# The first attention of a two-block network: stacked queries and keys, outputs already transposed, weights scaled by GpSimd

## What is computed

```python
s = jnp.einsum('btgrd,btgkd->btgrk', q_b, k_sel) * ATTN_SCALE
p = masked_softmax(s, mask)
...
g = jax.nn.sigmoid(gate_logits.astype(jnp.float32)).reshape(B, S, G, R, 3).astype(o_cmp.dtype)
o_nsa = g[..., 0:1] * o_cmp + g[..., 1:2] * o_sel + g[..., 2:3] * o_win
o_nsa = o_nsa.reshape(B, S, NSA_WIDTH) * jax.nn.silu(z_n)
...
o_dsa = o_dsa.reshape(B, S, DSA_WIDTH) * jax.nn.silu(z_d)
mixed = jnp.concatenate([o_nsa, o_dsa], axis=-1)
return x + jnp.einsum('bsc,cd->bsd', mixed, w_out)
```

## Time and profile before

| | |
|---|---|
| median of three runs | 1795.41 us |
| the profiled execution: its own time / span of the trace | 1794.89 us / 1793.1 us |
| busy: TensorE / VectorE / ScalarE / GpSimd | 97% / 55% / 41% / 39% |
| first turns of keys to the first score | 192.2 to 199.3 us |
| units of the first attention | 199.3 to 363 us |
| gate, turns, halves | 363 to 371.1 us |
| output projection `o1` | 371.1 to 425.5 us |

### The profile page before, as it was taken

One profiled execution on the slowest core, in us unless ns is written; L12 is line 12 of the kernel. 1 busy time (PEld: TensorE's weight loads), 2 busy tenths in 40 slices (PEclk: granted clock), 3 DMA queues, 4 the chain that ended last, 5 costly groups with the idle time before them and its releaser, 6 DMA issues. The chain is left out here.

```text
span 1793.1 us, 23296 instructions
## 1 busy us (share of the span) xinstructions
PE 1735.9 (97%) x8345; PEld 1416.5 (79%) x8345; DVE 990.4 (55%) x1657; ACT 741.1 (41%) x1282; POOL 694.3 (39%) x301
## 2 busy tenths in 40 slices
PE   7999998988999999999999999999999999999997
PEld 7777787777888777788888888887777888888886
DVE  5999776474579688633333335789775731111112
ACT  6434555523375564322222223466465343122321
POOL 3424111235430234555445557440211644444442
PEclk9999999999999999999999999999999999999998
DMA  7234010053332224455555532332310323232311
GB/s 251 82 106 141 24 36 25 24 194 121 109 101 100 83 83 149 146 193 192 189 193 194 188 141 94 108 103 84 106 37 24 106 94 100 90 104 94 99 54 47
DMA packets 56633, 197.65 MB, mean 110 GB/s; under 512 B 6993, under 2 KB 8017, under 8 KB 56530
## 3 DMA queue, kind: packets, MB, share of 16 engines
q1 hardware_dynamic: 55666, 194.15, 31.6%
q10 hardware_dynamic: 864, 2.11, 0.3%
HBM read 194.14 MB, written 2.10 MB: 109 GB/s over the span
## 5 line engine op out<-in xcount | busy, mean ns | idle before, releaser
L516 POOL TENSOR_TENSOR WL<-RAW,WH 128x1024 fp32r<-128x1024 f32 x234 | 593.9, 2543 | 872.6 <-ACT WH L600 535.9
L1917 PE MATMUL bank<-HH,WH 128*128 128x512 f32 x1120 | 439.0, 392 | 9.1 <-POOLq L521 5.4
L1919 PE MATMUL bank<-HH,WL 128*128 128x512 f32 x1120 | 437.7, 391 | 0.0
L1918 PE MATMUL bank<-HL,WH 128*128 128x512 f32 x1120 | 437.7, 391 | 0.0
L600 ACT ACTIVATE WH<-RAW 128x1024 fp32r<-128x1024 f32 x259 | 270.6, 1051 | 246.0 <-PE bank L1919 220.0
L1917 PEld LDWEIGHTS bank<-HH,WH 128*128 128x128 f32 x1120 | 211.5, 189 | 54.7 <-issue 8.0
L1919 PEld LDWEIGHTS bank<-HH,WL 128*128 128x128 f32 x1120 | 211.4, 189 | 44.1
L1918 PEld LDWEIGHTS bank<-HL,WH 128*128 128x128 f32 x1120 | 211.4, 189 | 43.6
L1837 DVE TENSOR_TENSOR HF<-SILU,bank 128x512 f32<-128x512 f32 x43 | 29.6, 688 | 301.6 <-PE bank L1919 300.6
L1917 PE MATMUL bank<-HDH,WH 128*128 128x512 f32 x352 | 137.1, 390 | 0.0
L1919 PE MATMUL bank<-HDH,WL 128*128 128x512 f32 x352 | 137.0, 389 | 0.0
(11 more groups left out here) (371 smaller groups left out, 2933.5 us busy)
## 6 DMA issues: line engine op xcount, KB each, us to landing
RAW<-in_stream SPq DMA_DIRECT2D x363, 512.0 KB, 3.3
out_t<-YA SPq DMA_DIRECT2D x8, 256.0 KB, 2.2
X<-in_xt ACTq DMA_DIRECT2D x3, 512.0 KB, 10.8
RAW<-in_stream SPq DMA_DIRECT2D x2, 256.0 KB, 3.9
X<-in_xt ACTq DMA_DIRECT2D x2, 256.0 KB, 6.0
ACC<-in_pos SPq DMA_DIRECT2D x1, 256.0 KB
gains<-in_gains SPq DMA_DIRECT2D x1, 224.0 KB
CS<-in_cs SPq DMA_DIRECT2D x1, 128.0 KB
```

The lines of the kernel that those rows point to most:

```text
L516: nc.gpsimd.tensor_tensor(lo(k)[:], raw(k)[:], hi(k)[:].bitcast(F32), ALU.subtract).then_inc(sem["passed"], mark("passed", *k))
L1917: nc.tensor.matmul(out, A[0], B[0], start=first, stop=False)
L1918: nc.tensor.matmul(out, A[0], B[1], start=False, stop=False)
L1919: return nc.tensor.matmul(out, A[1], B[0], start=False, stop=last)
```

## The change

- `UNITS1` goes head by head: four tiles of a head in one branch, then the other branch; the third branch last, head by head.
- The queries of a head are stored twice over 128 partitions, the rounded half on 64 and the rest on the other 64 (in `HH` and `HL`, free in this stage); a key head is stored as its rounded half on both 64s (in `WH`) and its rest on both (in `WL`). A score is two one-pass products. The compressed keys are done likewise (`KCS`).
- GpSimd scales each unit's weights by reciprocal sum and gate before they are turned (VectorE makes one reciprocal per unit); it also takes over the scaling of the first eight `ada` slots. The ring of weights grows from 4 to 8, the lags from 3 and 4 to 6 and 8.
- The values lie in `VZ` with 64 zero columns between heads, so that the output of a head can be added on either half of a bank. A pair of heads, both branches and the compressed branch gather in one bank (`pair_bank`), channels-first, from four products per head and branch.
- The gate `Z` is turned instead of the outputs (`GATE_TURN`), VectorE multiplies each finished pair with it, ScalarE and GpSimd (the last two: VectorE) make the halves.
- Of the turns before the loop only four stay; the others and the stacking are spread over the first 60 units (`TURNS`, `CONVERT`). Zeroing of `KT` (GpSimd) goes; `VZ` is zeroed at the kernel's start.
- The first two tiles of `o1` begin inside the loop (`O1_PARTS`); the sixteen `ada` slots beside `o1` all stand behind its third slot.

```diff
-        order += [ada.pop(0) for _ in range((2, 3, 3, 3, 3, 2, 0, 0)[n])]
+        order += [ada.pop(0) for _ in range((0, 0, 4, 4, 4, 4, 0, 0)[n])]
...
-UNITS1 = [(b, j, g, qt) for b in (0, 1) for j in range(4) for qt in range(NT) for g in range(2)]
-UNITS1 += [(2, j, g, qt) for qt in range(NT) for j in range(4) for g in range(2)]
+UNITS1 = [(b, h % 4, h // 4, qt) for h in range(HEADS) for b in (0, 1) for qt in range(NT)]
+UNITS1 += [(2, h % 4, h // 4, qt) for h in range(HEADS) for qt in range(NT)]
+RING1, T_LAG1, O_LAG1 = 8, 6, 8
...
+O1_PARTS = {101: ((0, 0, 3),), 102: ((0, 3, 5),), 103: ((0, 5, 7), (1, 0, 7), (0, 7, 8), (1, 7, 8))}
+GATE_TURN = {14 + 6 * c: c for c in range(KD)}
+TURNS = {5: ("tqn", 1), 8: ("tqn", 2), 11: ("tqn", 3), 13: ("tkc",)}
+TURNS.update({38 + 6 * j: ("tqd", j) for j in range(4)})
+CONVERT = {0: (("tk", 0, 1),), 1: (("tqn", 0, 1),), 2: (("tk", 1, 0),), 3: (("tk", 1, 1), ("tk", 2, 0)),
+           4: (("tk", 2, 1),), 13: (("tkc",),)}
+CONVERT.update({5 + 3 * (j - 1) + g: (("tqn", j, g),) for j in range(1, 4) for g in range(2)})
+CONVERT.update({38 + 6 * j + g: (("tqd", j, g),) for j in range(4) for g in range(2)})
...
+            for v in range(len(UNITS1)):
+                br, j, g, qt = UNITS1[v]
+                n = (qt + 1) * P
+                pool.wait_ge(sem["p_inv"], value("p_inv", v))
+                p_, over = PR[v % RING1][:, 0:n], COEF1[:, v % 16:v % 16 + 1]
+                if br == 2:
+                    ins = nc.gpsimd.tensor_scalar(p_, p_, over, ones[:, 0:1], ALU.mult, ALU.mult)
+                else:
+                    col = 3 * (4 * g + j) + 1 + br
+                    ins = nc.gpsimd.tensor_scalar(p_, p_, over, gate[:, qt, col:col + 1], ALU.mult, ALU.mult)
+                ins.then_inc(sem["p_pool"], mark("p_pool", v))
+                if v - 1 in ATT_ADA:
+                    pass_to(SLOT[("ada", 0, ATT_ADA.index(v - 1))] + 1)
...
+                if kind == "tk":
+                    k_hi, _ = key_stack(i, g)
+                    nc.scalar.activation(k_hi[rows_of(1 - g), :], b, ACT.Copy)
+                    ins = nc.scalar.activation(k_hi[rows_of(g), :], b, ACT.Copy)
+                else:
+                    ins = nc.scalar.activation(query_stack(kind, 4 * g + i)[rows_of(g), :], b, ACT.Copy)
...
-                    nc.tensor.matmul(b[:, 0:n], (QNT if br < 2 else QDT)[:, j, qt * P:(qt + 1) * P],
-                                     KT[:, 2 * br + g, 0:n], start=True, stop=False)
+                    for i, part in enumerate(key_stack(br, g)):
+                        nc.tensor.matmul(b[:, 0:n], query_stack(kind, 4 * g + j)[:, qt * P:(qt + 1) * P],
+                                         part[:, 0:n], start=(i == 0), stop=False)
...
-                        last = nc.tensor.matmul(b, PT1[:, v % RING, kb * P:(kb + 1) * P],
-                                                G[4][:, kb, c:c + DH], start=(kb == 0), stop=(kb == qt))
+                        last = nc.tensor.matmul(
+                            pair_bank[c][:, kb * P:S], VZ[:, kb, DH * m:DH * m + P], PT1[e % 2][:, kb, kb * P:S],
+                            start=(kb == 0 and NT * e == first),
+                            stop=(kb == NT - 1 and c >= 4 and NT * e + NT - 1 == end))
```

More of the change, by code:

```diff
@@ L227 @@
 RING = 4
-def evictor(v):
-    return "read_dve" if v % 4 == 3 else "read_act"
 UNITS2 = [(h, qt) for h in range(HEADS) for qt in range(NT)]
@@ L437, in first_square, with rows_of, query_stack, key_stack @@
             return (RELU[:, 0, :], RELU[:, 1, :], TMP[:, 0, :], TMP[:, 1, :])[k % 4]
+        def rows_of(g):
+            return slice(DH * g, DH * g + DH)
+        def query_stack(kind, h):
+            return (HH if kind == "tqn" else HL)[:, h, :]
+        def key_stack(br, g):
+            cols = slice(S * g, S * g + S)
+            return WH[KEY_SLOT[br]][:, cols], WL[KEY_SLOT[br]][:, cols]
+        def gated(c):
+            return Z[:, :, c * P:(c + 1) * P]
+        def chunked(x, c):
+            return x[:, c, :].rearrange("p (t q) -> p t q", t=NT)
         block = ctx.enter_context(nc.Block())
@@ L1511, in _ @@
+            pair_at = {pair_done(c) + 1: c for c in range(KD)}
             nU = len(UNITS1)
-            for u in range(nU + O_LAG):
+            for u in range(nU + O_LAG1):
                 if u < nU:
@@ L2156, in _, with turned @@
-            for i in range(4):
-                turn(("tqd", i), [G[3][:, tt, i * P:(i + 1) * P] for tt in range(NT)])
+            def turned(kind, i=0):
+                if kind == "tkc":
+                    pe.wait_ge(step, value("cmp_key"))
+                    turn(("tkc",), [CK[0:2 * NCMP, 0, :]], rows=DH)
+                    return
+                group = {"tk": 1, "tqn": 2, "tqd": 3}[kind]
+                pe.wait_ge(step, value("roped", group))
+                turn((kind, i), [G[group][:, tt, i * P:(i + 1) * P] for tt in range(NT)])
@@ new lines, in o1_part @@
+            def o1_part(n, k0, k1):
+                slot = ("o1", n)
+                if k0 == 0:
+                    o1_bank[n] = claim(*slot)
+                    pe.wait_ge(sem["passed"], value("passed", *slot))
+                for k in range(k0, k1):
+                    last = mm3(o1_bank[n][:], wpair(slot, P * k, P), mix_pair(k), k == 0, k == KD - 1)
+                if k1 == KD:
+                    full(last, *slot)
+                    used(slot)
+            o1_bank, pair_bank = {}, {}
@@ L2168, in _ @@
+            for u in range(nU + O_LAG1):
+                mods(("att", u))
+                if u in TURNS:
+                    turned(*TURNS[u])
+                c = GATE_TURN.get(u)
+                if c is not None:
+                    turn(("tz", c), [Z[:, tt, c * P:(c + 1) * P] for tt in range(NT)])
                 qt = cmp_tile(u, 0)
                 if qt is not None:
+                    pe.wait_ge(sem["read_dve"], value("read_dve", "tkc"))
                     for g in range(2):
@@ new lines, in _ @@
+                for c in range(4):
+                    if u == pair_done(c):
+                        if c == 0:
+                            pe.wait_ge(sem["read_act"], value("read_act", "ct", NT - 1))
+                        full(nc.tensor.matmul(pair_bank[c][:], VBLK[:, c // 2, P * (c % 2):P * (c % 2) + P],
+                                              PTC[:, c // 2, :], start=False, stop=True), "oc", c)
+                for n, k0, k1 in O1_PARTS.get(u, ()):
+                    o1_part(n, k0, k1)
@@ L2238, in _ @@
+            banks[0] = 8
             for n in range(KD):
-                dense(("o1", n), [(("o1", n), P * k) for k in range(KD)], mix_pair)
+                if n > 1:
+                    dense(("o1", n), [(("o1", n), P * k) for k in range(KD)], mix_pair)
                 mods(("o1", n))
```

368 lines of the change are left out of this document (204 added, 164 removed).

## The result

The changed kernel takes **1831.1 us** (median of four, 1826.8 to 1835.2), the kernel before 1796.1 beside it: ratio 1.0197, 95% interval 1.0172 to 1.0222. It is slower by 35 us; the forecast of 1774 missed by 57.

What follows compares the result with a forecast made beforehand. The prediction took TensorE's instruction list, plus about 10 us of waits, to bound the first attention. Its terms, -25.9 + 4.6 + 1.3 - 4.6 - 5 + 2.0 + 9.8 - 3 = -20.8 us, gave 1774 from 1794.9; range 1757 to 1789.

Steps and rivals of the forecast that it cites:

- Filling: First units of the attention loop: ScalarE's stacking leaves TensorE 7.8 us idle, plus 2 us for half clock; +9.8 us.
- Waits in the loop: First attention's loop: the others catch up during a head's block of output products, so fewer waits; -3 us.
- coupling rival: Loop: six banks leave less slack and every unit takes 0.16 us more, 15 us in all, 1789 us; chance 13%.
- Scores: First attention: two one-pass products per score, 1.30 us for four tiles in place of 2.38, 24 times; -25.9 us.
- Outputs: First attention: a head's output products take 2.25 us in place of 2.06, 24 times; +4.6 us.
- compressed scores: First attention: they stay 64 instructions, at 0.12 us each in place of 0.10; +1.3 us.
- Seam: Between attention and output projection: 8.1 us go, 32 gate turns of some 3.5 us move into the loop; -4.6 us.
- Projection: Output projection: clock stays at 1.0, two slots are split in advance, 4 us of waits left; -5 us.
- Start: Before the loop: first score at about 198.1 instead of 199.3, and 29 turns costing 3.2 us move behind it; +2.0 us.
- GpSimd's scaling: Loop: GpSimd scales each unit's weights in 0.33 to 0.76 us, costed at nothing; bounds 0 to +4 us.
- on GpSimd: Rival: GpSimd's scaling in every unit's chain becomes the bound; at 1.6 us a unit the kernel takes about 1815; chance 5%.
- slow products: Rival: one-pass products are no faster at these shapes, the scores' gain becomes 0 and the time 1800; chance 2%.

Runs made afterwards that it cites:

- e4: The changed kernel without the stacking of keys and queries in units 0 to 12, except the first key head and query; 1800.5 us, ratio 1.0018.
- e2: The changed kernel with VectorE making the low halves of a stack one unit later in units 0 to 9, behind the next maximum; 1820.6 us, ratio 1.0140.
- e1: The changed kernel with 60 filler products of TensorE in the holes of the first 12 units, written to banks nobody reads; 1833.4 us, ratio 1.0193.
- e9: The changed kernel with the second branch's late queries turned into the free output bank and their low halves made behind the next maximum; 1818.4 us, ratio 1.0136.
- e3: The changed kernel with the four output products of a head and branch spread over three units for the first 16 groups; 1825.1 us, ratio 1.0163.
- e13: The changed kernel with the edits of e4, e3, e9 and e12 together (stacking of the first units left out); 1776.2 us, ratio 0.9888.
- e12: The changed kernel with the modulation's slots beside the projection two or three at a time instead of four by four; 1830.5 us, ratio 1.0184.
- e7: The changed kernel with all eight banks in rotation until unit 11, instead of six; 1832.6 us, ratio 1.0203.
- e6: The changed kernel without GpSimd's 96 scalings of the weights (that work is left out); 1828.7 us, ratio 1.0186.
- e10: The changed kernel with the edits of e2, e3 and e9, third key stacked later, four banks until unit 4, two top-8 rounds moved into the loop; 1799.2 us.
- e14: e10 plus four key moves and table load ahead, e12's slot order, late queries turned two units later, first modulation turns five later; 1788.5 us, ratio 0.9957.

## Why the prediction was wrong

- **Filling (+9.8, bounds 3 to 13): the step that failed.** e4 puts the stacks of the first units at 30.6 us, or 25.1 by the trace. The key that I had ready for unit 4 at 206.3 is ready at 211.45, and unit 11, forecast at 213.8, is scored at 233.3. I had followed ScalarE's list by hand, moves and exponentials, and had let VectorE run beside it. In the order of the program VectorE's low halves stand ahead of the next maximum and wait for ScalarE's moves, and the next exponential waits for that maximum: nothing overlaps, 3.6 us from one exponential to the next with a key (of the 30.6, e2's order alone is 10.5). Both orders stood in the kernel's text; what was missing was to follow two in-order lists together. The half clock that I priced at 2 us lasted through most of the stretch, but it was free (e1).
- **Waits in the loop (-3, bounds +5 to -8): failed too, and by the trace this is the larger part.** From the first outputs to the last it takes 176.5 us, forecast 141; scores and outputs make 4.5 of these 35. Late stacks cost 12.7 us (e9), the outputs in a block 6.0 (e3), and with both mended and the first stacks gone e13's loop takes 149.2. I had noted the block and taken it for a place where the others catch up; they ran dry instead. A granted clock well below 1.0 in the loop, which I had named as a sign of being wrong, came: 0.89 from 240 to 360 us. The coupling rival named the six banks, as 0.16 us in every unit; the loss sat in few places, where a stack stands in the way, by its order or by the bank it holds (e9).
- **Scores (-25.9): mis-sized.** 1.58 us for four tiles make it 24 x (1.58 - 2.38) = -19.2. The first of the two products takes more than the second (0.15 against 0.11, 0.31 against 0.24), and I had read only the last one of a unit in the other attention.
- **Outputs (+4.6):** 2.16 in place of 2.25 us, +2.4. The compressed scores were right (16 products in 1.93 us).
- **Seam (-4.6): right.** The chain runs on without a gap: projection products begin at 405.85 and again at 411.45 directly behind the outputs, at a clock of 1.00 from 400 to 420 us. (At 3.22 us for 28 the 32 turns are 3.7 us, not 3.5.)
- **Projection (-5): the gain didn't come.** 51.9 us from the last outputs, and 3.5 for 15 products before them, 55.4 against 55 before. The waits of 4.8 us are those I left room for; what I counted on, a clock near 1.0, was 0.93. e12's order gets 3.9 of it in the stage, and nothing in the kernel's time.
- **Start (+2.0): near.** First score at 200.2, forecast 198.1; in kernels that leave the start alone it lay between 197.7 (e4) and 200.7 (e7), 199.3 in the mean.
- **GpSimd's scaling (0): right** (e6: 2.4 us less without it, within the noise).
- **Range and slack.** All bounds on the slow side together (+3.2, +8, +5, +4) give 1794, and the range ended at 1789. Three units of 1.44 us are 4.3 us of slack; the 3.7 of the coupling rival doesn't follow from them.

The slower side had 6%, most of it on GpSimd and 2% on slow products. It should have had the stacks: the one piece of new work that stands in a dependent chain while the pipeline is still empty. That e13 lands at the forecast is in part luck: its first outputs come 4 us earlier than forecast, since the filling is left out, and its loop takes 8 us longer, of which the scores are 6.7.

Open: whether in e9 the bank or the order did more; and why four executions of the changed kernel spread over 8 us, where four of the kernel before spread over 3. The two long ones (1835) have a mean granted clock of 0.972, the two short ones (1827) 0.975 and 0.978; what sets it isn't shown.

## What to carry to other kernels

When a change adds a step that crosses two in-order engines (one rounds, the other subtracts), follow both lists together at the place where it stands, and ask what the next item of each list waits for: a conversion that the pipeline doesn't need for many units belongs behind the next unit's work on the second engine, not ahead of it. A piece of data parked in a rotating bank shortens the rotation for everybody; park it in one that is out of the rotation (e9 shows the gain only together with a better order, and more banks alone, e7, brought nothing). And a half clock beside an idle TensorE is first of all a sign: look for the chain that it waits for before paying for filler.

## What the runs showed of the hardware

The granted clock of TensorE stayed near the lower level for most of 40 us while it was busy half of the time (20.1 of 40 us, 0.53), and filler products of bf16 in the holes brought it to 0.83 (27.4 of 40 us). From 240 to 360 us it was 0.89, and TensorE's longest waits there are the four of 15.4 us together. Behind the wait of 5.3 us at 312.91 a product of 384 columns takes 0.49 us to the next start, behind the one of 3.0 us at 327.87 the next such product (329.22) takes 0.26, as at full clock. The Trainium skill ("TensorE: Matmul & The Clock Gate", section "A second HAM failure mode: psum-queue depth-cycling") describes another case, a kernel whose clock swings since it cycles through banks and idles very briefly between groups of products; no run here shows that. An edit of order alone moved the clock of fixed stretches (which then hold other units) both ways: e3 brought 240 to 300 us from 0.89 to 0.97 and 300 to 360 from 0.89 to 0.83; e12 brought the projection from 0.93 to 1.00 and the 20 us behind it from 1.00 to 0.83.

The first exponential after the sine carried a load of its table. In e10, and then in e14, where an instruction of its own loads it ahead of the first exponential (but not ahead of the first maximum, 198.10):

```profile
199.58 1.28 ACT L944 ACT_TABLE_LOAD   x1 [2.00 <-PE bank L2359]
200.88 0.37 ACT L944 ACTIVATE PR<-bank,nmax 128x128 f32<-128x128 f32 x1
```

```profile
198.60 1.28 ACT L901 ACT_TABLE_LOAD   x1
199.90 0.20 ACT L901 ACTIVATE RSUM<-vec 128x1 f32<-128x1 f32 x1
200.11 0.37 ACT L949 ACTIVATE PR<-bank,nmax 128x128 f32<-128x128 f32 x1
```

1.28 us. "ScalarE activation tables: per-element evaluation and per-set limits" of the Trainium skill (section "What a function is on this engine") gives 1283 ns, and the trace agrees. "ScalarE: Activation LUTs" of the Trainium skill (section "What ACT_TABLE_LOAD costs") gives the same load and adds a drain of about 1380 ns to every switch, 2.66 us in all; the trace doesn't show it, since in e14 the instruction ahead of the load ends at 198.58 and the one behind it starts at 199.90, 1.32 us later.
